# Probability transposes and the product with v one attention step later, and first in a step's order on the matmul engine

## What is computed

```python
hn = rms_norm(x, norm_mix)                      # x: 1024 positions x 1024
proj = hn @ w_in + b_in
q, k = rope(rms_norm(q, q_norm)), rope(rms_norm(k, k_norm))
for g, (window, dilation) in enumerate(ATTN_PATTERNS):
    scores = q @ k.T * hd ** -0.5               # banded, per residue class of positions
    m = max(scores);  e = exp(scores - m);  den = sum(e)
    o_g = (e @ v) / den;  lse_g = m + log(den)
att = sum(softmax(lse)_g * o_g)
merged = sigmoid(gate_0) * (y_rnn @ w_o_rnn) + sigmoid(gate_1) * ((att * silu(z_att)) @ w_o_att)
x = x + merged @ w_out
x = x + sigmoid(rms_norm(x) @ w_ple_gate + b) * (p @ w_ple)
```

## Time and profile before

| | |
|---|---|
| Time, median of 3 runs | 1347.05 us (1346.85 to 1347.11) |
| The profiled execution's own time | 1346.43 us |
| Its span in the profile | 1344.6 us |
| Granted clock of the matmul engine | full speed in all 40 slices |
| Busy: VectorE, ScalarE, GpSimd | 59%, 38%, 40% |
| Attention steps in the span | first T at 335.0 us, last PV at 846.3 us |

### The profile page before, as it was taken

One profiled execution on the slowest core, in us unless ns is written; L12 is line 12 of the kernel. 1 busy time (PEld: TensorE's weight loads), 2 busy tenths in 40 slices (PEclk: granted clock), 3 DMA queues, 4 the chain that ended last, 5 costly groups with the idle time before them and its releaser, 6 DMA issues.

```text
span 1344.6 us, 17628 instructions
## 1 busy us (share of the span) xinstructions
PE 1330.4 (99%) x6254; PEld 1103.4 (82%) x6254; DVE 788.4 (59%) x1257; ACT 506.8 (38%) x1281; POOL 535.5 (40%) x500
## 2 busy tenths in 40 slices
PE   8999999999999999999999999999999999999998
PEld 6887888888888888888888888888888788888887
DVE  6799888842779666565665752159612466234323
ACT  7455646542434444344443688311200011223100
POOL 6975424404458334041340632353166317044020
PEclk9999999999999999999999999999999999999999
DMA  6232312332202032120320332376379545122111
GB/s 239 79 102 87 104 61 79 110 100 71 75 13 83 25 90 66 29 83 24 95 59 29 114 102 85 99 244 211 102 280 414 178 129 154 58 79 63 40 48 47
DMA packets 84470, 139.50 MB, mean 104 GB/s; under 512 B 10048, under 2 KB 41120, under 8 KB 84384
## 3 DMA queue, kind: packets, MB, share of 16 engines
q10 hardware_dynamic: 39936, 75.82, 15.9%
q1 hardware_dynamic: 44448, 62.56, 15.7%
HBM read 108.84 MB, written 29.51 MB: 103 GB/s over the span
## 4 chain that ended last, share of the span: by engine, by line
PE 86%; DVE 5%; DMA 5%; ACT 2%; issue 1%; POOL 0%; SPq 0%; ACTq 0%; POOLq 0%; DVEq 0%
PE bank L1257 26%; PE bank L1262 26%; PE bank L1261 26%; DMA g_in<-gate_dram 4%; PE bank L1407 2%; PE bank L1387 2%; PE bank L1374 1%; PE bank L1396 1%; DVE xc L991 1%; PE bank L1500 1%; DMA x_nat<-in_x 0%; ACT L736 0%; DVE ibuf L1018 0%; PE bank L1300 0%; DVE qkr L1099 0%
## 5 line engine op out<-in xcount | busy, mean ns | idle before, releaser
L539 POOL TENSOR_TENSOR ring<-raw,ring 128x512 fp32r<-128x512 f32 x221 | 311.8, 1411 | 724.7 <-PE bank L1262 642.3
L1257 PE MATMUL bank<-hn,ring 128*128 128x512 f32 x640 | 251.8, 393 | 2.3 <-DVE sgbuf L979 1.2
L1262 PE MATMUL bank<-hn,ring 128*128 128x512 f32 x640 | 249.4, 390 | 0.0
L1261 PE MATMUL bank<-hn,ring 128*128 128x512 f32 x640 | 249.2, 389 | 0.0
L1257 PE MATMUL bank<-ring,hn 128*128 128x512 f32 x576 | 232.6, 404 | 0.2 <-POOL ring L539 0.2
L1262 PE MATMUL bank<-ring,hn 128*128 128x512 f32 x576 | 225.8, 392 | 0.0
L1261 PE MATMUL bank<-ring,hn 128*128 128x512 f32 x576 | 225.2, 391 | 0.0
L543 POOL TENSOR_SCALAR ring<-raw 128x512 fp32r<-128x512 f32 x221 | 186.6, 844 | 8.2 <-DMA raw<-in_w_rnn_s 8.1
L1257 PEld LDWEIGHTS bank<-hn,ring 128*128 128x128 f32 x640 | 120.2, 188 | 27.4 <-DVE sgbuf L979 1.6
L1262 PEld LDWEIGHTS bank<-hn,ring 128*128 128x128 f32 x640 | 120.1, 188 | 25.4
L1261 PEld LDWEIGHTS bank<-hn,ring 128*128 128x128 f32 x640 | 120.2, 188 | 23.9
(11 more groups left out here) (181 smaller groups left out, 2157.4 us busy)
## 6 DMA issues: line engine op xcount, KB each, us to landing
raw<-in_w_tail_s SPq DMA_DIRECT2D x104, 256.0 KB, 2.7
g_in<-gate_dram ACTq DMA_DIRECT2D x48, 256.0 KB, 3.1
raw<-in_w_rnn_s SPq DMA_DIRECT2D x45, 256.0 KB, 2.7
raw<-in_w_qkv_s SPq DMA_DIRECT2D x48, 192.0 KB, 2.5
gate_dram<-g_out ACTq DMA_DIRECT2D x32, 256.0 KB, 2.1
raw<-in_w_qkv_s SPq DMA_DIRECT2D x48, 128.0 KB, 2.2
o_dram<-o_buf ACTq DMA_DIRECT2D x48, 128.0 KB, 1.8
o_in<-o_dram ACTq DMA_DIRECT2D x12, 512.0 KB, 3.7
```

Source lines behind the costliest of these rows:

```text
L539: nc.gpsimd.tensor_tensor(ring[:, ring_slot(p), 1], raw[:, p % RAW], ring[:, ring_slot(p), 0].bitcast(F32), ALU.subtract).then_inc(w_ready, 1)
L1257: ins = T.matmul(out, lhs[0], rhs[0], start=first, stop=False)
L1261: T.matmul(out, lhs[0], rhs[1], start=False, stop=False)
L1262: return T.matmul(out, lhs[1], rhs[0], start=False, stop=last)
```

## The change

The lags of the probability transposes and of the product with v grow from 5 and 6 steps to 6 and 7, so the steps are 103 instead of 102. On the matmul engine the two parts move from the end of a step to its beginning: the order is now ET, PV, T, QK. The lags are shared by all engines, so ScalarE's copies of bank 6 and bank 7 serve tiles A-6 and A-7 in step A; ScalarE's and VectorE's own order within a step is as before. No instruction is added or removed, and no buffer changes.

```diff
--- before.py
+++ after.py
@@ -86,7 +86,7 @@
 START = [("norm", t) for t in range(4)] + [("hn", n) for n in range(6)] + [("norm", 4), ("hn", 6), ("hn", 7)] \
     + [("norm", t) for t in range(5, NT)] + [("hn", n) for n in range(KD, 2 * KD)]
 
-LAG_T, LAG_QK, LAG_ET, LAG_PV = 2, 4, 5, 6
+LAG_T, LAG_QK, LAG_ET, LAG_PV = 2, 4, 6, 7
 STEPS = TILES + LAG_PV
 FIRST_STEP, STEP_BLOCKS = 90, 6
 STEP_AT = {FIRST_STEP + STEP_BLOCKS * A: A for A in range(STEPS)}
@@ -1363,6 +1363,27 @@
 
 
             def attention(A):
+                g = A - LAG_ET
+                if 0 <= g < TILES:
+                    grp, tile = g // (HEADS * NT), g % NT
+                    pe.wait_ge(exp_done, g + 1)
+                    if g >= 1:
+                        pe.wait_ge(etc_done, g)
+                    for b in ((0, 1) if has_prev(grp, tile) else (1,)):
+                        ins = T.transpose(bank[6][:, b * P:(b + 1) * P], scores[:, g % 2, b * P:(b + 1) * P], ident[:])
+                    ins.then_inc(et_done, 1)
+                g = A - LAG_PV
+                if 0 <= g < TILES:
+                    grp, tile = g // (HEADS * NT), g % NT
+                    c, vb = part_of(g // NT, 2)
+                    pe.wait_ge(etc_done, g + 1)
+                    if g >= 1:
+                        pe.wait_ge(ot_done, g)
+                    parts = (0, 1) if has_prev(grp, tile) else (1,)
+                    for b in parts:
+                        ins = T.matmul(bank[7][:, 0:P], qkv[:, c % 3, tile if b else prev_tile(grp, tile), vb],
+                                       probsT[:, g % 2, b * P:(b + 1) * P], start=b == parts[0], stop=b == 1)
+                    ins.then_inc(pv_done, 1)
                 g = A - LAG_T
                 if 0 <= g < TILES:
                     if g == 0:
@@ -1386,27 +1407,6 @@
                         keys = qkT[:, 1].rearrange("p (n c q) -> p c n q", n=2, c=4)[:, tile % 4]
                     T.matmul(bank[5][:, 0 if prev else P:2 * P], qkT[:, 0, tile * P:(tile + 1) * P],
                              keys, start=True, stop=True).then_inc(qk_done, 1)
-                g = A - LAG_ET
-                if 0 <= g < TILES:
-                    grp, tile = g // (HEADS * NT), g % NT
-                    pe.wait_ge(exp_done, g + 1)
-                    if g >= 1:
-                        pe.wait_ge(etc_done, g)
-                    for b in ((0, 1) if has_prev(grp, tile) else (1,)):
-                        ins = T.transpose(bank[6][:, b * P:(b + 1) * P], scores[:, g % 2, b * P:(b + 1) * P], ident[:])
-                    ins.then_inc(et_done, 1)
-                g = A - LAG_PV
-                if 0 <= g < TILES:
-                    grp, tile = g // (HEADS * NT), g % NT
-                    c, vb = part_of(g // NT, 2)
-                    pe.wait_ge(etc_done, g + 1)
-                    if g >= 1:
-                        pe.wait_ge(ot_done, g)
-                    parts = (0, 1) if has_prev(grp, tile) else (1,)
-                    for b in parts:
-                        ins = T.matmul(bank[7][:, 0:P], qkv[:, c % 3, tile if b else prev_tile(grp, tile), vb],
-                                       probsT[:, g % 2, b * P:(b + 1) * P], start=b == parts[0], stop=b == 1)
-                    ins.then_inc(pv_done, 1)
 
             def positions(grp, tile, w):
```

## The result

The changed kernel takes 1357.44 us in the median (1355.95 to 1357.98), the kernel before 1347.08: ratio 1.0073, 95% interval 1.0062 to 1.0085, **10.4 us slower**. The prediction was 1352.1 in a range of 1348.0 to 1355.5. The sign was right; the loss was twice what was forecast, and the time lies 1.9 us above the range.

A forecast was written before the change was run, and what follows sets the result against it. The matmul engine, 99% busy, was taken to bound the kernel; +3.41 + 0.04 + 1.7 = +5.1 us on the profiled 1346.43 gave 1351.5, and 0.62 up to the median 1352.1 us, range 1348.0 to 1355.5.

The forecast's parts named there:

- Which wait binds: At ET: the copy freeing bank 6 comes after the exponential, so it sets the five stalls, 2.27 us in sum.
- Rival A: At ET: the exponential binds, so the lag removes all waits, -2.3 us, 1344.8 us; chance 0.08.
- Part 2: ET first in its step waits longer for late bank-6 copies: 5.68 against 2.27 us, +3.41, and a seventh place +0.04.
- Part 3: T and QK last start VectorE's maximum up to 0.67 us later, delaying ScalarE's copies: +1.7 us, bounds 0 and 4.7.
- 4 x 0.3: Shift allowed at four late places in the upper bound for late T and QK: 0.4 + 1.3 + 4 x 0.3 = 2.9 us.
- rival D: VectorE's turns lost to GpSimd cascade: +8.1 us and more, 1355.2 us upwards; chance 0.12.
- Part 1: ET one step later: its exponential wait goes, the bank-6 wait stays, so nothing comes off the binding wait.
- Part 4: Matmul engine: the same 6,254 matmuls, each short one about 0.11 us whatever is beside it; 0 us.
- Rival B: A wide QK at the step's end covers the first projection matmul's weight load: -3.9 us, 1348.2 us; chance 0.12.
- C: ET's waits vanish and the projection's weight load is covered, so the kernel gets faster: 1340.9 us; chance 0.04.
- Rival E: Some stalls shrink because a stalled step gives ScalarE time: total under +2.7 us, 1349 us; chance 0.04.
- Part 5: One more step at the end and later output writes: cost 0, at most a step's 5.5 us once.

## Why the prediction was wrong in size

**Which wait binds: right.** ET starts 0.14 us after the copy of bank 6 in after, as it started 0.15 after it in before, with the exponential a step older. Rival A (the exponential binds) is refuted.

**Part 2, ET first, +3.45 us: right in kind.** ET first waits for every late copy from the step's start on. Putting it first with QK nearly in place gave +3.8 us, but that the number comes so near is in part luck: some copies had moved, and the waits of that kernel sum to 7.0 us and not to the 5.7 priced.

**Part 3, T and QK last, +1.7 of at most 4.7: the step that failed.** From the ten waits it is 11.49 - 5.68 - 0.04 = 5.8 us, above my upper bound. In the order of time the excess over the copies of before is 0.64, 0.25, -0.06, 0.33, 1.24, 0.49, 0.73, 1.10, 0.49, 0.56 us. What was off:

- The lost turn. I gave it to the step at 417.76, behind the stretch of permutes, where nothing came (-0.06): VectorE was behind already, and by the step ahead of it the delay was gone (the maximum starts 1.56 us after its step's start, 1.63 before). It came at 480.70 and 652.91 instead, 1.24 and 1.10 us. I had the first at 0.04 with at most 0.55 of shift, and the second only in a lump for steps that just escape. In rows 7 the copy was ready at the very start of the step, so a whole lost turn came through as a wait; that row said how little was in reserve, and I priced it by a shift.
- Absorption. I took row 527.18 of rows 8, a rotation already held, as the common picture. It tells what happens if that instruction starts later, not whether a later one will meet GpSimd as well. And the shift itself was larger than I had it: where a narrow QK stands behind the PV of a wide tile, as before the waits of 1.68 and 1.42, the maximum comes 0.55 us later and not 0.3, and nearly all of it arrived (0.49 each). At 593.74 and 763.15 more arrived than the delay: 0.34 us of the maximum became 0.73 and 0.56.
- The bound. "4 x 0.3" took the delay of QK as the most that could arrive in the narrow steps, while the sentence before had said that a turn costs 1.3. The upper bound should have been a turn at every late place. The measured total lies in rival D (+8.1 and more), which had 0.12. But no cascade made it: two places lost a whole turn, 2.3 us together, and the other eight gave 3.4.

The rule of the port pair, cited there from the Trainium skill (SBUF — State Buffer, "SBUF: two separate sides"), allowed a lost turn. The experiments agree with it: with a shorter one-input instruction on GpSimd the distance shrinks to 3.8 us.

**Part 1, the lag costs nothing: wrong by itself,** though it did not add to the sum. The lags alone cost 3.9 us, by the traces through the wait of the maximum for the ET that empties its `scores` buffer; no run took this wait away alone. In the changed kernel ET stands ahead of QK, so this wait ends first.

**Part 4, order on the matmul engine, 0: right,** the step is 1.32 us long in both. Rival B (a covered weight load) and with it C are refuted: after a wide QK the projection matmul starts earlier, 0.25 us behind QK's first row, but its successor comes 0.42 behind it, so nothing is won. Rival E (a total under 2.7) did not come.

**Part 5: right,** no wait appears outside the steps.

## What to carry to other kernels

When an instruction waits for two things, lengthening its lag helps only against the one that ends last; here that was the buffer behind it, and the order of ScalarE's own step set it. Move the copy that frees a buffer ahead of the slow part (a table load), and then the lag pays: -2.8 us, where the lag and order alone cost 10.

Before something is moved back in a step, follow who waits for it to the next shared resource. On a chain that alternates with another engine, a delay needn't arrive as itself. Here it came as nothing, as a part, as more than itself or as a whole turn of 1.2 us, so its upper bound is a turn at each place without reserve.

And after a change of lags, list again every wait on a reused buffer: one that pointed to the step before may now point to the same step.

## What I had not expected of the hardware

VectorE and GpSimd can start together: at 469.10 both do, the rotation takes its 0.42 us and GpSimd's subtraction 1.58 instead of 1.28; a rotation that comes 0.26 us behind is held and takes 1.40. At this place a delay of the maximum by 0.32 us is enough to turn the one into the other, and one of 0.21 us is not. Elsewhere an instruction of 0.11 us made a copy 1.37 us later.
